# A scan's gate products put among its state updates, four norms' sums shared out anew, and a low half made earlier

## The chip, the cores and the metric

One kernel runs on one core of a Trainium2 chip. The metric is the device time of one execution in microseconds (us); lower is better. All work is in one launch. TensorE multiplies, VectorE, ScalarE and GpSimd do the elementwise work, and SyncE issues the large loads.

## The reference, cut to what matters

The reference is a chain of two blocks on 256 tokens of width 1024, with a context of 256 tokens beside them. The first block has a token mixer (a gated linear scan in two directions and a long convolution, merged under gates) and a mixture of 32 experts. The second has two layers of a hybrid mixer with a squared-relu MLP. Norms stand between all of them:

```python
def rms_norm(x, g):
    xf = x.astype(F32)
    y = xf * lax.rsqrt(jnp.mean(xf * xf, axis=-1, keepdims=True) + EPS)
    return (y * g.astype(F32)).astype(x.dtype)

def gla_chunk_scan(q, k, v, log_f, s0):          # in chunks of 32 tokens
    def step(S, xs):
        ...
        o = (jnp.einsum('bhtk,bhkv->bhtv', qc * jnp.exp(bc), S)
             + jnp.einsum('bhts,bhsv->bhtv', scores, vc))
        S_new = (jnp.exp(total[:, :, 0, :])[..., None] * S
                 + jnp.einsum('bhsk,bhsv->bhkv', kc * jnp.exp(total - bc), vc))
        return S_new, o

def merge_branches(y_a, y_b, g_logits, w_pa, w_pb, w_o):
    g_a, g_b = jnp.split(g_logits, 2, axis=-1)   # g_logits: part of h @ w_in
    mixed = jax.nn.sigmoid(g_a) * (y_a @ w_pa) + jax.nn.sigmoid(g_b) * (y_b @ w_pb)
    return mixed @ w_o
```

The scan has 4 heads of 128 and 8 chunks in each direction. The gate logits are 2048 of the columns of h @ w_in, which don't depend on the scan.

## The kernel before, in words

Five engine programs are written out by hand and are ordered by semaphores alone. At the end of each of fourteen stages every engine drains and waits for the others (`phase_end`). Weights come in chunks of 2 MB (512 columns or rows) through a ring of four slots; SyncE loads a chunk into a slot once TensorE has said that the slot's last chunk was used, and TensorE waits for a chunk with `chunk_in`. An fp32 matmul of the trace is two records. Where a product is needed in full precision from cheaper passes, both operands are split into a high and a low half (`mm3`: high x high, high x low, low x high).

*The scan* (stage `scan_b`, lines 740 to 797). For each of two directions d, TensorE turns the keys, makes scores (which VectorE masks out of banks 6 and 7 into SC, semaphore `masked`) and the context state (copied by VectorE, L2145, semaphore `states_out`). Then two halves bi follow, of four chunks each. A half begins with its state updates: for each chunk j a group of four matmuls on the 32 rows of this chunk, rows 32j to 32j + 31, into bank j. In the first half the products of masked scores and values follow (the "intra" products). Then for each chunk n the query product with the state before it (128x32, semaphore `inter`) waits until VectorE has made that state (L2153, L2154, `states_out`), and four products of a gate tile follow it (`gate_part`, 128 rows by 256 columns, banks 6 and 7). The gate tiles of a direction are 4 tiles of 8 products. In the second direction VectorE also does a part of the short convolution between two states (L2132 to L2134).

*The norms.* A norm (`mean_root`, then `norm`) needs the sum over the eight 128-row blocks of the squares. ScalarE squares a block once its residual has been added (L1380, semaphore `squares`). GpSimd adds blocks 1 to 5 into block 0 (`add_squares`, L1847, semaphore `squares_added`), and `sums` on TensorE multiplies blocks 0, 6 and 7 with a matrix of ones. Call 0 is the first norm; calls 1, 4, 5, 6 and 7 are the first block's second norm, layer 0's second, layer 1's first and second, and the final one. Calls 0, 4 and 5 are 512 wide, the others 256. TensorE's sums are followed by a stage end, except in the last call, where they precede the output.

*The low half.* In layer 1 the first two weight chunks of the input projection are split ahead: ScalarE copies four high halves (L1826) between its squares at the end of layer 0, VectorE makes the first chunk's two low halves there (L2627), and the second chunk's two low halves (L2417) behind the whole norm of layer 1, before it goes on to split the third chunk. TensorE waits for them at the second projection (`chunk_in(n + 1)`).

Of the kernel before, what the change touches and what calls it, by code (L numbers as in the profile page):

```python
# [30 lines left out]
L = 256  # L31
# [120 lines left out]
def build(nc, T, out):  # L152
    ctx = ExitStack()
    with ctx:
# [372 lines left out]
        W1h_cols, W2h_rows = W1h.rearrange("p (k n) -> p k n", k=KT), W2h.rearrange("p (k n) -> p k n", k=4)  # L527

        AHEAD = 3
        REST = [(k, 0) for k in range(AHEAD)] + [(k, s) for k in range(AHEAD, KT) for s in (1, 0)]  # L530
# [26 lines left out]
        def _(pe):  # L557
# [28 lines left out]
            def chunk_in(n, turns=0):  # L586
                pe.wait_ge(full[n % RING], arrived(n) + turns)
# [16 lines left out]

            def sums(call, nth, n, bank=6):

                pe.wait_ge(S("squares_added"), 5 * nth)
                for k in (0, KT - 2, KT - 1):
                    if k:
                        pe.wait_ge(S("squares"), 8 * call + k + 1)  # L610
                    mm(ps[bank][:, 0:n], ones, H[:, k, 0:n], k == 0, k == KT - 1, "sum_ready" if k == KT - 1 else None)
# [51 lines left out]
            ada_turn(1, 7, 1)  # L663
            sums(0, 1, 2 * L, 1)
            ada(2, 2, 6, blk=0)
# [73 lines left out]
            for d in range(2):  # L739
# [24 lines left out]
                for h in range(HG_H):  # L764
                    for tb in range(2):
                        mm(ps[0][:, h * P:(h + 1) * P], KDN[:, tb * 4 + h, :], Vn[:, 2 + tb, h * P:(h + 1) * P], tb == 0, tb == 1,
                           "ctx_state" if (h, tb) == (3, 1) else None)

                chunk_in(win(8 + d))
                pe.wait_ge(S("turned_out"), 4 * d + 4)  # L770
                pe.wait_ge(S("states_out"), 8 * d + 1)
                for bi in range(2):
                    tb = bi if d == 0 else 1 - bi
                    if bi:
                        pe.wait_ge(S("states_out"), 8 * d + 5)
                    for j in range(4):
                        r = slice(32 * j, 32 * j + 32)
                        for h in range(HG_H):
                            mm(ps[j][:, h * P:(h + 1) * P], KEN[r, tb * 4 + h, :], Vn[r, tb, h * P:(h + 1) * P],
                               inc="updates" if (j, h) == (3, 3) else None)  # L780
                    if bi == 0:
                        pe.wait_ge(S("masked"), 2 * d + 2)
                        for h in range(HG_H):
                            for tb2 in range(2):
                                mm(ps[4 + h // 2][:, (h % 2) * L + tb2 * P:(h % 2) * L + (tb2 + 1) * P],
                                   Vn[:, tb2, h * P:(h + 1) * P], SC[d][:, tb2 * 4 + h, :], False, False)
                    for c in range(4):
                        n = 4 * bi + c
                        ch = n if d == 0 else 7 - n
                        pe.wait_ge(S("states_out"), 8 * d + n + 1)  # L790
                        for h in range(HG_H):
                            mm(ps[4 + h // 2][:, (h % 2) * L + ch * 32:(h % 2) * L + ch * 32 + 32],
                               ST[:, n % 4, h * P:(h + 1) * P], QD[d][:, h, ch * 32:ch * 32 + 32], False, False,
                               "inter" if h == 3 else None)
                        gate_part(8 + d, n // 2, range(4 * (n % 2), 4 * (n % 2) + 4))
                chunk_used()
# [85 lines left out]
            for t in range(2, KT):  # L882
# [5 lines left out]
                if t % 4 == 3:  # L888
                    chunk_used()
            sums(1, 2, L)  # L890
            phase_end(pe, "merged")
# [157 lines left out]
            for l, first, mlp in ((0, L0, MLP0), (1, L1, MLP1)):  # L1049
# [215 lines left out]
                for t in range(2, KT):  # L1265
# [5 lines left out]
                    if t % 4 == 3:  # L1271
                        chunk_used()
                sums(ncall, 3 + 2 * l, W)
                ncall += 1
# [72 lines left out]
                flush()  # L1347
                sums(ncall, 4 + 2 * l, W)
                ncall += 1
# [483 lines left out]
        def _(pool):  # L1833
# [7 lines left out]
            def add_squares(call, n):  # L1841
                for k in range(1, KT - 2):
                    pool.wait_ge(S("squares"), 8 * call + k + 1)
# [112 lines left out]
        def _(dve):  # L1956
# [399 lines left out]
            with dve.If(more > 0):  # L2356
                with dve.Fori(0, more) as q:
                    dve.wait_ge(S("over_begun"), q * NX + 1)
                    V.tensor_scalar(RKM, RKM, -float(CAP), None, ALU.add).then_inc(S("over_ranked"), 1)
                    with dve.Fori(0, NX) as e:  # L2360
# [8 lines left out]
                        V.tensor_copy(SWT[0:CAP, :], ps[4][0:CAP, 0:L]).then_inc(S("over_weights"), 1)  # L2369
            dve.wait_ge(S("experts_done"), 1)  # L2370
            def split_chunk(n, c=KT * 512):

# [34 lines left out]
            for l in range(LAYERS):  # L2407
                W = 2 * L if l == 0 else L
                first = (L0, L1)[l]
                if l:  # L2410
                    norm(ncall, 1 + l, 0, (0, 1))
                    ncall += 1
                    n = L1 + 2
                    for a in range(2):
                        s = slice(2048 * a, 2048 * (a + 1))
                        dve.wait_ge(S("high_copied"), 12 + 2 + a + 1)
                        i = V.tensor_tensor(low(n)[:, s], slot(n)[:, s], NEXTh[2 + a].bitcast(F32), ALU.subtract)  # L2417
                    i.then_inc(full[(n + 1) % RING], 16)
                for j in range(1 + l, 5):
# [228 lines left out]
                if l == 0:  # L2648
# [3 lines left out]
                    link(V.tensor_tensor(mod[:, 2, 6:48, :], mod[:, 2, 6:48, :], bc(vecs[:, lo + 6:lo + 48].unsqueeze(2), [P, 42, 2]), ALU.add))  # L2652
                    gains(2)
                    phase_end(dve, "l0_mlp")
            dve.wait_ge(S("rms_ready"), ncall + 1)
# [64 lines left out]
```

## Time and profile before

| | us |
|---|---|
| median of 3 runs | 1965.12 (1961.49 to 1965.41) |
| the profiled execution | 1964.91 |
| its span, first to last instruction | 1963.1 |
| TensorE busy, share | 1869.2, 95% |
| VectorE busy, share | 817.9, 42% |
| ScalarE busy, share | 586.2, 30% |
| GpSimd busy, share | 389.0, 20% |

The stages that the change touches lie at 218 to 298 us (the scan), and the norms' sums at 402, 1183, 1544, 1763 and 1955 us. The stretch from about 440 to 870 us belongs to the experts, where the DMA engines move 427 GB/s. PEclk is the granted TensorE clock: 1.00 is 2.4 GHz and 0.50 is 1.2 GHz. A row of the timeline is start, duration, engine, line, operation, operands and count; a bracket behind it is the idle time of the engine before it and what ended that.

### The profile page before, as it was taken

What the parts mean: (1) busy time and instruction counts of PE and PEld (TensorE: products, weight loads), DVE (VectorE), ACT (ScalarE), POOL (GpSimd) and SP (SyncE); (2) the same over time, 40 slices, a digit from 0 to 9 for tenths busy, and PEclk for the clock granted to TensorE, in tenths of its full rate; (3) what the DMA queues carried; (4) which work ended last, traced back from release to release, by engine and by line L of the source; (5) the groups of instructions that cost most, each with busy time, mean ns of one, the idle gap of its engine ahead of it and who ended that gap; (6) DMA issues with size and microseconds to landing.
All of it is one profiled execution on the core that took longest, in us unless ns stands there. A gap on an engine that the chain in (4) does not pass through costs nothing.

```text
span 1963.1 us, 26165 instructions
## 1 busy us (share of the span) xinstructions
PE 1869.2 (95%) x11248; PEld 1369.8 (70%) x11248; DVE 817.9 (42%) x1342; ACT 586.2 (30%) x892; POOL 389.0 (20%) x205
## 2 busy tenths in 40 slices
PE   6999999999999999989999899999999899889998
PEld 2777796964443443437887657888888688779998
DVE  2625245731111111116342844556555625574333
ACT  2523103331111111114112535222333411544554
POOL 2000000120000000006002032433343250025665
PEclk9999999989999999999999999999999899999999
DMA  9569817569999999992224004345444232414551
GB/s 358 181 241 363 313 44 278 204 264 428 427 427 427 428 426 427 427 413 94 86 86 141 23 33 171 140 166 188 150 150 152 92 122 87 174 53 163 175 198 37
DMA packets 111425, 429.84 MB, mean 219 GB/s; under 512 B 5706, under 2 KB 8821, under 8 KB 98512
## 3 DMA queue, kind: packets, MB, share of 16 engines
q1 hardware_dynamic: 109056, 416.56, 54.7%
q0 software_dynamic: 2256, 11.62, 1.6%
q8 instruction: 90, 1.47, 0.3%
q14 instruction: 23, 0.19, 0.0%
HBM read 427.11 MB, written 1.05 MB: 218 GB/s over the span
## 4 chain that ended last, share of the span: by engine, by line
PE 66%; DMA 16%; DVE 6%; PEld 5%; ACT 3%; issue 3%; PEldq 0%; POOL 0%; SPq 0%; POOLq 0%; DVEq 0%; ACTq 0%
PE bank L562 65%; DMA ring<-in_moe_w_down 7%; PEld bank L562 5%; DMA H<-in_moe_w_down 4%; DMA arena<-in_moe_w_down 4%; PE bank L577 1%; DVE H L1989 1%; DVE H_low L1996 1%; PEldq L541 0%; DMA ring<-in_w_in 0%; DMA arena<-in_hy_filt_w 0%; DVE arena L2514 0%; DVE ring_low L2590 0%; DVE ring_low L2171 0%; DVE ring_low L2584 0%
## 5 line engine op out<-in xcount | busy, mean ns | idle before, releaser
L562 PE MATMUL bank<-arena_r 128*128 128x256 f32 (+1 forms) x2176 | 592.0, 339 | 12.0 <-ACT arena_r L1386 6.5
L562 PE MATMUL bank<-arena_r,ring_low 128*128 128x512 f32 (+2 forms) x1920 | 596.5, 342 | 1.7 <-DVE H_low L1996 1.0
L562 PEld LDWEIGHTS bank<-arena_r 128*128 128x128 f32 x2176 | 385.1, 190 | 63.8 <-issue 15.9
L562 PE MATMUL bank<-arena 128*128 128x64 bf16 (+8 forms) x2892 | 366.7, 320 | 39.9 <-DMA arena<-in_hy_filt_w 11.5
L562 PEld LDWEIGHTS bank<-arena_r,ring_low 128*128 128x128 f32 (+1 forms) x1920 | 352.7, 188 | 47.6 <-issue 2.7
L562 PEld LDWEIGHTS bank<-arena 128*128 128x128 bf16 (+4 forms) x2892 | 207.5, 133 | 199.8 <-issue 170.7
L562 PE MATMUL bank<-H_low,arena_r 128*128 128x512 f32 (+1 forms) x672 | 217.1, 340 | 0.0
L562 PE MATMUL bank<-ring,arena 128*64 128x512 f32 x768 | 170.2, 599 | 8.5 <-DMA ring<-in_moe_w_down 8.5
L2572 DVE SCALAR_TENSOR_TENSOR X<-bank,mod,X 128x256 f32<-128x256 f32 x216 | 94.2, 478 | 196.6 <-PE bank L562 196.6
L1928 POOL TENSOR_TENSOR ring_low<-ring,arena_r 128x2048 fp32r<-128x2048 f32 x31 | 142.4, 4614 | 131.2 <-DVE ring_low L2584 68.8
L1400 ACT ACTIVATE arena<-bank 128x512 f32<-128x512 f32 (+2 forms) x106 | 51.2, 496 | 368.1 <-PE bank L562 367.9
L2344 DVE SCALAR_TENSOR_TENSOR arena_r<-bank,arena,arena_r 128x512 fp32r<-128x512 f32 x32 | 24.0, 750 | 307.2 <-ACT arena_r L1586 307.2
L1944 POOL TENSOR_TENSOR arena_r<-arena,arena_r 128x512 fp32r<-128x512 f32 (+1 forms) x64 | 104.6, 1647 | 222.4 <-ACT arena L1806 222.4
L562 PEld LDWEIGHTS bank<-ring,arena 128*64 128x64 f32 x768 | 56.5, 138 | 115.1 <-issue 115.0
L562 PEld LDWEIGHTS bank<-H_low,arena_r 128*128 128x128 f32 x672 | 125.5, 192 | 14.3
L2640 DVE SCALAR_TENSOR_TENSOR arena<-ring,arena 128x1024 f32<-128x1024 f32 x84 | 99.5, 1222 | 66.0 <-POOL arena_r L1944 62.5
L562 PE MATMUL bank<-H,arena 128*64 128x512 f32 (+4 forms) x464 | 118.0, 436 | 7.4 <-DVE arena L2530 2.8
L562 PE MATMUL bank<-X,ring 128*128 128x256 f32 x512 | 118.1, 386 | 0.0
L562 PEld LDWEIGHTS bank<-X,ring 128*128 128x128 f32 x512 | 96.5, 192 | 17.8 <-issue 4.7
L1799 ACT ACTIVATE arena_r<-ring 128x4096 fp32r<-128x4096 f32 x15 | 54.5, 3631 | 172.4 <-DMA ring<-in_w_mlp 123.3
L562 PE MATMUL bank<-H_low,ring_low 128*128 128x512 f32 (+2 forms) x272 | 93.4, 358 | 0.0
L1884 POOL CAST ring_low<-ring 128x4096 fp32r<-128x4096 f32 x1 | 3.6, 3598 | 450.5 <-DMA ring<-in_w_in 450.5
(326 smaller groups left out, 1939.3 us busy)
## 6 DMA issues: line engine op xcount, KB each, us to landing
ring<-in_w_mlp SPq DMA_DIRECT2D x32, 2048.0 KB, 7.9
ring<-in_w_in SPq DMA_DIRECT2D x26, 2048.0 KB, 8.9
ring<-in_ada_w SPq DMA_DIRECT2D x24, 2048.0 KB, 12.2
ring<-in_moe_w_up SPq DMA_DIRECT2D x17, 2048.0 KB, 23.2
ring<-in_moe_w_gate SPq DMA_DIRECT2D x17, 2048.0 KB, 27.9
arena<-in_moe_w_up SPq DMA_DIRECT2D x15, 2048.0 KB, 22.5
ring<-in_moe_w_down SPq DMA_DIRECT2D x14, 2048.0 KB, 23.4
arena<-in_moe_w_down SPq DMA_DIRECT2D x13, 2048.0 KB, 23.5
```

Source lines behind the costliest of these rows:

```text
L562: ins = nc.tensor.matmul(o, l, r, start=start, stop=stop, skip_group_check=True)
L577: ins = nc.tensor.transpose(o, i, ident)
L1400: A_(o, i, f, **kw).then_inc(S("tile_free"), 1)
L1799: A_(W2h, slot(n), ACT.Copy).then_inc(S("w_high"), 1)
L1884: G.tensor_copy(low(L0 + 1), slot(L0)).then_inc(S("pool_ready"), 1)
L1928: G.tensor_tensor(low(n)[:, s], slot(n)[:, s], W1h[:, s].bitcast(F32), ALU.subtract).then_inc(S("w1_split"), 1)
L1944: G.tensor_tensor(HAl[:, nt, 0:W], HA[:, nt, 0:W], HAh[:, nt, 0:W].bitcast(F32), ALU.subtract)\
L1989: V.scalar_tensor_tensor(H[:, k, c], X[:, k, c], gsc[:, b, which, k, s:s + 1], root[:, c], ALU.mult, ALU.mult)\
L1996: return V.scalar_tensor_tensor(Hl[:, k, c], H[:, k, c], mod[:, b, 24 * which + k, s:s + 1], high[:, k, c].bitcast(F32), ALU.add, ALU.subt ...
L2344: V.scalar_tensor_tensor(YSl[:, s], ps[6 + nb][:, :], WSL, YSh[:, s].bitcast(F32), ALU.mult, ALU.subtract)\
L2572: i = V.scalar_tensor_tensor(X[:, t, s * L:(s + 1) * L], o[:, s * L:(s + 1) * L], mod[:, 1 + l, gate + t, s:s + 1], X[:, t, s * L:(s + 1) ...
L2640: d = V.scalar_tensor_tensor(CPROD[:, c, :], as_turned(n)[:, q % 3, :], 1.0, CSIL[:, c, :], ALU.mult, ALU.mult, accum_out=mod[:, 2, bass.d ...
```

## The change

Three things change. In the scan the gate products of a direction are handed out by an iterator in the same order as before: two ahead of the wait for the first state (behind the chunk's arrival and the wait for the mask, which moves up), one behind each of the four groups of updates of a half, and three or two (not four) behind each query product. In all calls of the sums but the first, GpSimd adds blocks 1 to 3 instead of 1 to 5, and TensorE sums blocks 0, 4, 5, 6 and 7. In layer 1, one low half of the second chunk is made by VectorE at the end of layer 0 (behind the gains, before the stage end), and the other ahead of the norm instead of behind it.

```diff
+        def blocks_added(call):
+            return KT - 2 if call == 0 else KT - 4
+        def added_before(call):
+            earlier = {0: (), 1: (0,), 4: (0, 1), 5: (0, 1, 4), 6: (0, 1, 4, 5), 7: (0, 1, 4, 5, 6)}[call]
+            return sum(blocks_added(c) - 1 for c in earlier)
...
-            def sums(call, nth, n, bank=6):
-                pe.wait_ge(S("squares_added"), 5 * nth)
-                for k in (0, KT - 2, KT - 1):
+            def sums(call, n, bank=6):
+                m = blocks_added(call)
+                pe.wait_ge(S("squares_added"), added_before(call) + m - 1)
+                for k in (0, *range(m, KT)):
                     if k:
                         pe.wait_ge(S("squares"), 8 * call + k + 1)
                     mm(ps[bank][:, 0:n], ones, H[:, k, 0:n], k == 0, k == KT - 1, "sum_ready" if k == KT - 1 else None)
...
+                gates = iter([(nt, k) for nt in range(4) for k in range(KT)])
+                def gate_products(m):
+                    for _ in range(m):
+                        nt, k = next(gates)
+                        gate_part(8 + d, nt, (k,))
                 chunk_in(win(8 + d))
+                pe.wait_ge(S("masked"), 2 * d + 2)
+                gate_products(2)
                 pe.wait_ge(S("turned_out"), 4 * d + 4)
                 pe.wait_ge(S("states_out"), 8 * d + 1)
                 for bi in range(2):
...
                         for h in range(HG_H):
                             mm(ps[j][:, h * P:(h + 1) * P], KEN[r, tb * 4 + h, :], Vn[r, tb, h * P:(h + 1) * P],
                                inc="updates" if (j, h) == (3, 3) else None)
+                        gate_products(1)
                     if bi == 0:
-                        pe.wait_ge(S("masked"), 2 * d + 2)
...
-                        gate_part(8 + d, n // 2, range(4 * (n % 2), 4 * (n % 2) + 4))
+                        gate_products(3 if n < 6 else 2)
...
             def add_squares(call, n):
-                for k in range(1, KT - 2):
+                for k in range(1, blocks_added(call)):
...
+            def next_low(a):
+                s = slice(2048 * a, 2048 * (a + 1))
+                dve.wait_ge(S("high_copied"), 12 + 2 + a + 1)
+                return V.tensor_tensor(low(L1 + 2)[:, s], slot(L1 + 2)[:, s], NEXTh[2 + a].bitcast(F32), ALU.subtract)
...
                 if l:
+                    next_low(1).then_inc(full[(L1 + 3) % RING], 16)
                     norm(ncall, 1 + l, 0, (0, 1))
                     ncall += 1
-                    n = L1 + 2
-                    for a in range(2):
-                        s = slice(2048 * a, 2048 * (a + 1))
-                        dve.wait_ge(S("high_copied"), 12 + 2 + a + 1)
-                        i = V.tensor_tensor(low(n)[:, s], slot(n)[:, s], NEXTh[2 + a].bitcast(F32), ALU.subtract)
-                    i.then_inc(full[(n + 1) % RING], 16)
...
                     gains(2)
+                    next_low(0)
                     phase_end(dve, "l0_mlp")
```

The callers of `sums` lose their `nth` argument.

## Rows read from the trace of the kernel before

**Rows 1.** The page: TensorE's busy time, and its granted clock in 40 slices.
```profile
PE 1869.2 (95%) x11248; PEld 1369.8 (70%) x11248; DVE 817.9 (42%) x1342; ACT 586.2 (30%) x892; POOL 389.0 (20%) x205
...
PEclk9999999989999999999999999999999899999999
```

**Rows 2.** The page: the chain that ended last, by engine.
```profile
PE 66%; DMA 16%; DVE 6%; PEld 5%; ACT 3%; issue 3%; PEldq 0%; POOL 0%; SPq 0%; POOLq 0%; DVEq 0%; ACTq 0%
```

**Rows 3.** TensorE's timeline in the scan: start, us, what, count [idle before, releaser].
```profile
229.91 2.79 PE L562 MATMUL bank<-arena 32*128 32x128 f32 x32 [0.87 <-DVE arena L2145]
...
236.95 1.97 PE L562 MATMUL bank<-X,ring 128*128 128x256 f32 x8
...
263.47 1.95 PE L562 MATMUL bank<-H 128*128 128x128 f32 x16
...
284.54 0.38 PE L562 MATMUL bank<-X,ring 128*128 128x256 f32 x1
284.85 2.82 PE L562 MATMUL bank<-arena 32*128 32x128 f32 x32
287.59 1.08 PE L562 MATMUL bank<-H,arena 128*128 128x32 f32 x8
288.51 1.97 PE L562 MATMUL bank<-X,ring 128*128 128x256 f32 x8
...
288.81 0.38 PE L562 MATMUL bank<-X,ring 128*128 128x256 f32 x1
```

**Rows 4.** TensorE's waits in the scan: total us, times, longest.
```profile
PE bank L562 <- DVE arena L2145: 1.7, 2, 0.9
```

**Rows 5.** Stretches: us, PE busy, PEld, DVE, ACT, POOL, granted clock, DMA share, GB/s.
```profile
233.00:236.50 3.50, 3.50 (x19) 3.50 (x19) 3.19 (x6) 0.00 (x0) 0.00 (x0) 0.51 1.05 388
...
250.10:253.60 3.50, 3.50 (x11) 2.96 (x11) 3.22 (x6) 0.00 (x0) 0.00 (x0) 0.51 0.00 0
...
270.60:274.00 3.40, 3.40 (x17) 3.18 (x16) 2.84 (x6) 0.00 (x0) 0.00 (x0) 0.50 0.12 40
274.00:298.20 24.20, 24.20 (x164) 21.94 (x162) 15.86 (x30) 1.15 (x3) 0.00 (x0) 1.00 0.00 1
```

**Rows 6.** Timeline of VectorE: the last state of the second direction.
```profile
294.10 0.69 DVE L2154 TENSOR_TENSOR arena<-arena,bank 128x512 f32<-128x512 f32 x1
```

**Rows 7.** TensorE's timeline: the sums of the first block's second norm.
```profile
402.00 1.03 PE L562 MATMUL bank<-H,base 128*128 128x256 f32 x4
403.19 0.70 PE L562 MATMUL bank<-H,base 128*128 128x256 f32 x2 [0.16 <-ACT H L1380]
```

**Rows 8.** TensorE's timeline: the sums of layer 0's second norm.
```profile
1182.74 2.92 PE L562 MATMUL bank<-H,base 128*128 128x512 f32 x6
```

**Rows 9.** Timelines of all engines about layer 1's first norm.
```profile
1542.30 1.65 ACT L1380 ACTIVATE H<-X 128x512 f32<-128x512 f32 x3
1543.00 1.27 POOL L1847 TENSOR_TENSOR H<-H 128x512 f32<-128x512 f32 x1 [1.05 <-ACT H L1380]
...
1544.32 4.26 PE L562 MATMUL bank<-H,base 128*128 128x512 f32 x6 [3.27 <-POOL H L1847]
...
1550.13 1.67 DVE L1989 SCALAR_TENSOR_TENSOR H<-X,gsc,RS 128x256 f32<-128x256 f32 x4 [7.60 <-ACT RS L1377]
...
1562.81 4.48 DVE L2417 TENSOR_TENSOR ring_low<-ring,arena_r 128x2048 fp32r<-128x2048 f32 x2
...
1567.39 0.47 PE L562 MATMUL bank<-arena_r 128*128 128x512 f32 x1 [1.50 <-DVE ring_low L2417]
```

**Rows 10.** The stretch in which the first projection of layer 1 begins.
```profile
1550.60:1557.40 6.80, 5.70 (x27) 5.73 (x28) 6.80 (x19) 4.43 (x10) 0.00 (x0) 0.50 0.00 1
```

**Rows 11.** Timelines about layer 1's second norm.
```profile
1762.78 1.56 PE L562 MATMUL bank<-H,base 128*128 128x256 f32 x6 [0.40 <-POOL H L1847]
...
1765.49 0.47 ACT L1376 ACTIVATE RS<-bank,vecs 128x256 f32<-128x256 f32 x1 [2.14 <-DVEq L541]
```

**Rows 12.** TensorE's timeline: the sums of the final norm.
```profile
1954.62 1.62 PE L562 MATMUL bank<-H,base 128*128 128x256 f32 x6
```

More of the change, by code:

```diff
@@ L663, in _ @@
             ada_turn(1, 7, 1)
-            sums(0, 1, 2 * L, 1)
+            sums(0, 2 * L, 1)
             ada(2, 2, 6, blk=0)
@@ L889, in _ @@
                     chunk_used()
-            sums(1, 2, L)
+            sums(1, L)
             phase_end(pe, "merged")
@@ L1272, in _ @@
                         chunk_used()
-                sums(ncall, 3 + 2 * l, W)
+                sums(ncall, W)
                 ncall += 1
@@ L1347, in _ @@
                 flush()
-                sums(ncall, 4 + 2 * l, W)
+                sums(ncall, W)
                 ncall += 1
```

## The prediction

> **What bounds the kernel now.** I read the page's busy table and its forty slices first: TensorE works in 95% of the span, at the full clock in nearly every slice [rows 1]. The chain of waits agrees: 66% of it is TensorE, 16% is DMA, most of it in the experts' stage, which is not touched [rows 2]. So a saving counts where TensorE either waits or runs at the lower clock, and a cost counts where it adds passes or breaks the packing of its passes. Everything between the scan and the experts is ordered by semaphores from TensorE's own progress, the loads included (a slot is loaded once it is used), and so is what follows; I let every shift pass through to the end. In the trace each fp32 matmul is two records, which I call passes.
>
> **The scan, the largest part.** Four blocks of state updates (two directions, two halves) have 32 passes each on 32 rows, in four groups of eight, one group for each row quarter. The change puts one gate product (two passes, 128 rows, 256 columns) behind each group.
>
> *Packing.* Passes of one kind come every 0.11 us where they can't overlap: the sixteen score passes take 1.95 us less the last one's 0.28, over fifteen intervals. Thirty-two would then need 31 x 0.111 = 3.45 us from the first start to the last, and a start behind passes of another kind adds 0.1 (as 288.51 to 288.81 for the first two gate passes, where the later ones stand 0.215 apart: 288.81 to 288.51 + 1.97 - 0.38 = 290.10, six intervals). The block takes less: it starts at 284.85 and its last pass starts at 284.85 + 2.82 - 0.27 = 287.40, so 2.55 us. The difference, 1.0 us, is three boundaries between groups at 0.33 us: the next quarter's first passes run beside the last ones of the quarter before. A full-height gate product between them leaves nothing to run beside. On top of that each change between 32 and 128 rows costs time in both directions: the last gate pass starts at 284.54 and the first update at 284.85, 0.31 us instead of 0.215; from the last update at 287.40 to the next 128-row pass it is 0.19; and the first gate pass to the second takes 0.30 [rows 3]. One group followed by one product, up to the next group, is therefore 0.88 (seven intervals and the slower start) + 0.19 + 0.30 + 0.31 = 1.68 us; now a group inside a block takes 2.55 less 0.88, over three = 0.56, and a product 0.43, together 0.99. Each of the three inner insertions costs 0.7 us, the fourth nothing (the change of height is there already). Four blocks: 12 x 0.7 = **+8.4 us**. The bounds are 0 (if the products slip in as they do among themselves) and 12 x 0.8; I take the value of the rows, since both transitions stand in them.
>
> The Trainium skill speaks against the change here: TensorEngine Tiling (Array Packing), Key Properties, says that different tiles can load and multiply in parallel, and that changing the tiling mode makes TensorE drain. By this rule every change pays a drain; the trace agrees with its 0.31 and 0.19 us.
>
> *Idle time.* Before the first block of each direction TensorE waits for the first state to be copied, 0.87 us twice [rows 3, 4]. Two products (0.95 us) now stand there. The mask they must wait for is made while TensorE still computes the context state, and the chunk's wait stood here already; behind both waits on TensorE are the updates, for which VectorE waits, and they start no later than now. **-1.7 us.**
>
> *The clock.* Three stretches of 3.4 us are at 1.2 GHz, each right behind a block of updates: granted clock 0.51, 0.51 and 0.50; about the fourth block it is 1.00 [rows 5]. From the first update of the first block to its first gate pass it takes 7.04 us (229.91 to 236.95), against 2.74 (284.85 to 287.59) + 1.88 (16 passes of 128 columns, with a slower start) + 0.82 (287.59 to 288.51 less 0.1) = 5.44 at the full clock [rows 3]: 1.6 us lost; I use it for each of the three. If the clock stays up this is **-4.8 us**. It should: the mix of gate passes and light 128x32 passes behind 274 never loses the clock, nor does the fourth block at 284.85, which directly follows a run of gate products; and the new block has two full-height passes for eight updates throughout. It is not certain, for this mix stands in no row and lies between those that kept the clock and those that lost it.
>
> The skill's TensorE: Matmul & The Clock Gate, Why this matters for your kernels, ties throughput drops to long idle gaps between bursts. By that alone the scan has nothing to regain, since TensorE is busy through the low stretches with at most 0.87 us of idle time ahead of them, and the sum would be 4.8 us higher. The trace disagrees: the clock falls after low-row work with no idle time.
>
> *The states.* VectorE builds the states of the second direction with a convolution between them; the last is ready at 294.10 + 0.69 = 294.79, 7.4 us behind the last update pass [rows 3, 6]. TensorE now reaches the last state after 0.2 + 0.5 (product four) + 3 x 0.83 (inter passes) + two runs of three products at 1.38 and one of two at 0.95 = 6.9 us. It will wait some 0.5 us. **+0.5 us.** Earlier states are in time, since the block's end signal, the states and the queries behind it all shift together.
>
> Scan: 8.4 - 1.7 - 4.8 + 0.5 = **+2.4 us**.
>
> **The norms.** In the five later norms GpSimd adds three squares instead of five, TensorE sums five blocks instead of three: four passes more. It pays only where GpSimd is late.
> - *First block's second norm:* four passes run while square 7 is made, then two [rows 7]. Two of the four new passes fit before 403.19; the last pass moves from 403.51 to 402.00 + 9 x 0.215 = 403.94. **+0.4 us.**
> - *Layer 0, second norm (512 wide):* the six passes stand closely, the last starts at 1182.74 + 2.92 less its own 0.6, at 1185.07 [rows 8]; ten at 0.43 put it at 1186.6. **+1.5 us.**
> - *Layer 1, first norm:* here GpSimd is late. Its last add waits for square 5 and ends at 1544.27; TensorE idles 3.27 us and then starts cold: six passes in 4.26 us [rows 9]. Now the adds end before the last MLP tile does; blocks 0 and 4 go at once (from about 1541.1, where TensorE falls idle now), and 5, 6, 7 follow their squares (three in 1.65 us from 1542.30). Ten passes at 0.43, 0.1 for the start and the last one's tail end at about 1545.7, not 1548.58: 2.9 us earlier. The first low half (2.2 us, half of the row's 4.48) starts when VectorE is free, 7.60 us ahead of 1550.13, is ready at about 1544.8 and hides; the high copy that it reads is ahead of squares 5 to 7 on ScalarE. The second (2.2 us) starts with the new phase at 1545.8 and ends near 1548.1, later than the root (1547.3), so the norm starts at 1548.1 for 1550.13: 2.0 us earlier. The first projection ends 2.0 earlier too, at 1567.39 - 1.50 - 2.0 = 1563.9, and the second follows at once where it waited for the two low halves until 1567.39 [rows 9]: **-3.5 us**. Its bounds: -2 or less if the first half is late and holds the phase, and -5.2 if the low clock of this stretch (0.50 for 6.8 us [rows 10]) is halved.
> - *Layer 1, second norm:* the phase waits for VectorE's low half. ScalarE starts the root at 1765.49, released by VectorE, while the sums end at 1764.34 [rows 11]; four passes of 0.215 more end at 1765.2. **0**, and at the worst +0.9 us.
> - *Final norm:* nothing waits for GpSimd, and nothing hides the four passes: 4 x 0.215 less a short wait [rows 12]. **+0.8 us.**
>
> Norms: 0.4 + 1.5 - 3.5 + 0.8 = **-0.8 us**.
>
> **The sum.** 2.4 - 0.8 = +1.6 us on the profiled execution's 1964.91 (span 1963.1): 1966.5. The median of the runs shown, 1965.12, is 0.2 above it: **1966.7 us**, no change that can be told. What a measurement of this kernel can tell from no change is about 0.2%, or 3.9 us.
>
> **The rivals.**
> - *The clock stays low in the new blocks (slower).* Place: the four update blocks, now 6 us long each. Price: the 4.8 us are not regained and the fourth block loses 1.6 as well: +1.6 + 6.4 = +8.0, 1973 us; up to 1979 if a block holds two low stretches. It decides from the point where a group and its product, with the gaps of the two changes of height, no longer keep the granted clock at 1.00. For: those gaps are new. Against: the fourth block kept the clock with gate passes only ahead of it.
> - *The products cost little among the updates (faster).* Then the 8.4 us shrink: at a third of it (the transitions without the lost overlap) the total is +1.6 - 5.6 = -4.0, 1961 us; at nothing -6.8, 1958 us. The extra 1.7 us of the layer 1 stretch pulls the same way. Against: the overlap is in the trace and needs neighbouring quarters.
> - *The norm gains little.* The change does not do what it says if the first low half ends after TensorE's sums, or if GpSimd's three adds are late: then -3.5 becomes about -1 and the total +4.1, 1969 us. For: 1 us of slack only. Against: VectorE has been idle since 1542.5.
>
> **Numbers.** My forecast 0.45 (spread -2 to +4 about it), the low clock 0.22, cheap insertion 0.2, weak norm 0.13. The forecast itself spills a little over either bound: faster by over 0.2% is 0.17, within 0.2% 0.46, slower 0.37. The range 1959.5 to 1974 leaves out the far end of the low-clock case and of free insertion.
>
> **What would show it.** Groups of updates about 1.7 us apart with a product between, and a first block from first to last update near 5.9 us instead of 2.55; granted clock 1.00 throughout the scan; no wait for the copied first state and a short one for the last state of the second direction; the scan's end about 2 us later. In the norms: no idle of TensorE on GpSimd ahead of the layer 1 norm, and the second projection right behind the first. I am wrong if updates and products keep an interval near 1.0 us per pair, or if the clock row shows low stretches inside the blocks.

## The result, and the profile after

The changed kernel takes 1983.28 us (median of 4 runs, 1981.41 to 1985.54) against 1965.23 us before (1961.49 to 1965.41): a ratio of 1.0084, 95% interval 1.0061 to 1.0106, so 12 to 21 us slower. The forecast was 1966.7 us with a range up to 1974; the time lies outside it. The profiled execution has a span of 1983.2 us, 20.1 us more than before's 1963.1.

The page of the changed kernel: busy time, granted clock by slices, chain of waits [rows 1, 2].

```profile
PE 1897.0 (96%) x11268; PEld 1386.4 (70%) x11268; DVE 816.5 (41%) x1342; ACT 586.2 (30%) x892; POOL 378.8 (19%) x195
...
PEclk9999978989999999999999899999999999999999
...
PE 69%; DMA 15%; DVE 5%; PEld 5%; ACT 3%; issue 3%; PEldq 0%; POOL 0%; SPq 0%; ACTq 0%; DVEq 0%; POOLq 0%
```

TensorE has 20 passes more (1.8 thousandths of its passes) but 27.8 us more busy time, so its passes have become slower on the whole. The clock row says where: slices 6 and 7 (248 to 347 us) stand at 7 and 8, where 9 stood. I split the 20.1 us at events that both traces have. Up to the scan's first update -0.5; **the scan, from its first update to the first pass behind it, 87.24 us for 68.94: +18.3**; to the first block's second norm +0.1; through that norm and the experts +2.8; to layer 0's second norm +1.2; to layer 1's second norm (layer 1's first norm lies in it) -3.2; to the final norm +0.6; the rest +0.8.

The scan in TensorE's timeline (columns as [rows 3]; line 571 is before's line 562):

```profile
228.34 1.03 PE L571 MATMUL bank<-X,ring 128*128 128x256 f32 x4
229.38 1.12 PE L571 MATMUL bank<-arena 32*128 32x128 f32 x8
230.44 0.70 PE L571 MATMUL bank<-X,ring 128*128 128x256 f32 x2
231.07 1.15 PE L571 MATMUL bank<-arena 32*128 32x128 f32 x8
...
234.49 1.26 PE L571 MATMUL bank<-arena 32*128 32x128 f32 x8
235.68 1.22 PE L571 MATMUL bank<-X,ring 128*128 128x256 f32 x2
```

Two products stand ahead of the first block with no idle time, then a group comes every 1.71 us (231.07 to 234.49 is two periods). The product behind the fourth group takes 1.22 us for two passes that took 0.70 before: there the clock has fallen. The next view shows how much of the scan runs that way. Stretches of the changed kernel (columns as [rows 5]; the last one is the whole scan):

```profile
229.38:235.40 6.02, 6.02 (x38) 4.66 (x38) 0.00 (x0) 0.00 (x0) 0.00 (x0) 1.00 1.05 388
235.40:238.80 3.40, 3.40 (x15) 3.00 (x14) 2.76 (x4) 0.00 (x0) 0.00 (x0) 0.50 0.80 293
252.50:262.70 10.20, 10.20 (x36) 8.38 (x36) 4.14 (x6) 0.38 (x1) 0.00 (x0) 0.50 0.00 0
279.80:290.00 10.20, 10.20 (x41) 9.26 (x40) 8.58 (x16) 0.38 (x1) 0.00 (x0) 0.50 0.00 1
300.30:310.50 10.20, 10.20 (x36) 8.38 (x35) 5.34 (x10) 0.39 (x1) 0.00 (x0) 0.50 0.00 0
229.38:316.62 87.24, 86.72 (x460) 74.03 (x460) 30.52 (x53) 5.14 (x12) 0.00 (x0) 0.80 0.18 63
```

34.0 us of the scan are at the lower level (0.50, 1.2 GHz), where before it was 10.3 us [rows 5]; its mean clock is 0.80, and TensorE is busy in 86.72 of the 87.24 us. The blocks themselves hold the smaller part of this. These are the passes at the end of the second and of the third block and behind them:

```profile
254.31 2.07 PE L571 MATMUL bank<-arena 32*128 32x128 f32 x8
256.32 1.22 PE L571 MATMUL bank<-X,ring 128*128 128x256 f32 x2
257.33 1.75 PE L571 MATMUL bank<-arena 128*128 128x32 f32 x8
258.90 2.91 PE L571 MATMUL bank<-X,ring 128*128 128x256 f32 x6
...
280.90 1.22 PE L571 MATMUL bank<-X,ring 128*128 128x256 f32 x2
281.91 5.17 PE L571 MATMUL bank<-H,arena 128*128 128x128 f32 x24
286.89 2.91 PE L571 MATMUL bank<-X,ring 128*128 128x256 f32 x6
```

In each block the clock falls during the third or fourth group, or just behind the last update (at 235.40 in the first block). Up to the end of each block's fourth product (236.70, 257.33, 281.91 and 305.74) the low time adds up to about 14 us; the other 20 us run on through the intra products, the queries and the gate products that follow.

What TensorE waits for, from 225 to 320 us (columns as [rows 4]): no state any more, in place of before's 1.7 us.

```profile
PE bank L571 <- ACTq L550: 0.5, 1, 0.5
PE bank L571 <- DVE mod L1995: 0.5, 1, 0.5
PE bank L571 <- ACT arena L1532: 0.2, 1, 0.2
```

The sums of the five later norms, in order [rows 7, 8, 9, 11, 12]:

```profile
419.86 2.32 PE L571 MATMUL bank<-H,base 128*128 128x256 f32 x10
...
1204.62 4.45 PE L571 MATMUL bank<-H,base 128*128 128x512 f32 x10
...
1564.54 4.75 PE L571 MATMUL bank<-H,base 128*128 128x512 f32 x10
...
1781.47 2.32 PE L571 MATMUL bank<-H,base 128*128 128x256 f32 x10
...
1973.90 2.42 PE L571 MATMUL bank<-H,base 128*128 128x256 f32 x10
```

None waits for GpSimd, and the third one starts with no idle time, where before TensorE idled 3.27 us. About it, on VectorE and then on TensorE, the two low halves, the norm, and the second projection [rows 9]; the last row is ScalarE's root in layer 1's second norm [rows 11]:

```profile
1565.95 2.29 DVE L2394 TENSOR_TENSOR ring_low<-ring,arena_r 128x2048 fp32r<-128x2048 f32 x1
1569.44 2.29 DVE L2394 TENSOR_TENSOR ring_low<-ring,arena_r 128x2048 fp32r<-128x2048 f32 x1 [1.20 <-PEq L550]
1571.65 1.67 DVE L2008 SCALAR_TENSOR_TENSOR H<-X,gsc,RS 128x256 f32<-128x256 f32 x4
...
1586.58 0.47 PE L571 MATMUL bank<-arena_r 128*128 128x512 f32 x1 [0.21 <-ACT arena L1419]
...
1784.74 0.47 ACT L1395 ACTIVATE RS<-bank,vecs 128x256 f32<-128x256 f32 x1 [2.14 <-DVEq L550]
```

### The profile page after: what moved, and what is told of

It is laid out like the page before. It is cut to its first block, busy times and chain, and to the rows that moved or that the text cites. A ratio compares the mean times of both kernels' runs of the same rounds, so it can differ in the third digit from the quotient of the medians.

```text
span 1983.2 us, 26187 instructions
## 1 busy us (share of the span) xinstructions
PE 1897.0 (96%) x11268; PEld 1386.4 (70%) x11268; DVE 816.5 (41%) x1342; ACT 586.2 (30%) x892; POOL 378.8 (19%) x195
## 4 chain that ended last, share of the span: by engine, by line
PE 69%; DMA 15%; DVE 5%; PEld 5%; ACT 3%; issue 3%; PEldq 0%; POOL 0%; SPq 0%; ACTq 0%; DVEq 0%; POOLq 0%
PE bank L571 68%; DMA ring<-in_moe_w_down 7%; PEld bank L571 5%; DMA H<-in_moe_w_down 4%; DMA arena<-in_moe_w_down 3%; PE bank L586 1%; PEldq L550 0%; DMA ring<-in_w_in 0%; DMA arena<-in_hy_filt_w 0%; DVE arena L2534 0%; DVE ring_low L2610 0%; DVE H L2008 0%; DVE ring_low L2190 0%; DVE ring_low L2604 0%; DVE ring_low L2084 0%
## 5 line engine op out<-in xcount | busy, mean ns | idle before, releaser
L571 PE MATMUL bank<-arena 128*128 128x64 bf16 (+8 forms) x2892 | 381.4, 323 | 38.2 <-DMA arena<-in_hy_filt_w 11.7
L571 PEld LDWEIGHTS bank<-arena 128*128 128x128 bf16 (+4 forms) x2892 | 218.1, 135 | 205.2 <-issue 173.7
L571 PE MATMUL bank<-X,ring 128*128 128x256 f32 x512 | 128.5, 402 | 0.0
L571 PE MATMUL bank<-ring_low,arena_r 128*128 128x512 f32 x288 | 92.8, 394 | 0.0
```

The costliest lines, as they stand in the source:

```text
L571: ins = nc.tensor.matmul(o, l, r, start=start, stop=stop, skip_group_check=True)
```

## The experiments

The theory: the loss is the lower clock that one product per group lets in; packing costs what the prediction says. The rival: the insertions themselves cost more than foreseen, or a wait does. "The scan" below is always the stretch from the first update to the first pass behind the scan, in the run's one profiled execution, and whole times are medians. Numbers in brackets behind a ratio are its 95% interval. The comparison's kernel before had 1965.2 to 1966.0 us.

**The scan's part and the norms' part, each alone.** The first takes the hunks on the gate products, the second those on the sums and the low half; nothing else is edited.

> Only the scan's part of the change (products ahead, one behind each group, three or two behind each query); norms and low halves as before. Theory A (the low clock inside the update blocks carries the loss; the lost packing is the 0.7 us per inner insertion that the forecast had): about 17 us slower than before, with 7 to 10 stretches of 3.4 us at 1.2 GHz between the first update and the scan's end, and groups of updates 1.7 us apart wherever the clock is full. Rival B (the loss comes from the norms or from the experts' stage, which took 2 us more in the changed kernel): below 10 us slower.

> Only the sums and the low halves; the scan as before. Theory A: faster by 1 to 3 us (+0.4, +1.5, -4 to -5, 0, +0.8 as the trace of the changed kernel has them). Rival B: slower by 2 us or more, because the four added passes cost in five places and the gain of layer 1 is undone later. The experts' stage (last pass of the first block's second norm to the transposes behind the experts) within 1 us of before if its 2.4 us in the changed kernel were chance; 2 us longer if the later sums cause them.

The scan's part alone: 1983.54 us, ratio 1.0079 (1.0051 to 1.0107), scan 87.24 us, the same to a hundredth. The norms' part alone: 1963.76 us, 0.9994 (0.9978 to 1.0010), scan 68.95 us. The whole loss is in the scan. Its stretch with the scan's part alone:

```profile
231.51:318.75 87.24, 86.72 (x461) 74.08 (x461) 30.52 (x53) 5.14 (x12) 0.00 (x0) 0.80 0.17 63
```

**Two products behind each group, and none.** The kernel is the one with the scan's part alone (the norms as before), and only the counts change:

```diff
-                        gate_products((1, 1, 1, 1)[j])
+                        gate_products((2, 2, 2, 2)[j])
...
-                        gate_products((3, 3, 3, 3, 3, 3, 2, 2)[n])
+                        gate_products((2, 2, 2, 2, 2, 2, 1, 1)[n])
```

The other kernel has no product inside a block, and (4, 4, 4, 4, 4, 4, 3, 3) behind the queries.

> The scan's part alone, but two gate products behind each group instead of one (2 ahead, 8 in each half, then two, at the end one, behind each query). The lost packing is the same as with one product: 12 inner insertions of 0.7 us. Theory A (what was mis-sized is the clock: one product a group is too little to keep it, two are enough): granted clock 1.00 through the scan, a period of 2.1 us from group to group, and the scan about 2 to 4 us longer than before, total within 1 to 5 us of before. Rival B (products among low-row passes bring the clock down whatever their number): low stretches in the blocks as with one product, 10 us or more slower than before.

> The scan with whole update blocks as before; only two gate products stand ahead of the first state's wait, and four or three follow each query. Theory A: the 0.87 us waits of TensorE go (-1.7 us) and nothing else is lost; the clock behind the blocks falls in about as many places as before, so -2 us, with 1.6 us more or less for each low stretch fewer or more. Rival B (the early wait for the mask or the later queries cost the gain): no change or slower.

With two products behind each group: 1972.20 us, 1.0023 (1.0007 to 1.0039). With none: 1962.82 us, 0.9988 (0.9971 to 1.0005). Both scans as stretches, two products first:

```profile
231.61:305.49 73.88, 72.08 (x460) 61.42 (x460) 30.54 (x53) 5.14 (x12) 0.00 (x0) 0.98 0.21 74
```

```profile
231.05:293.37 62.32, 61.81 (x460) 56.85 (x460) 30.52 (x53) 5.14 (x12) 0.00 (x0) 1.00 0.25 88
```

Sixteen more products among the updates make the scan 13.4 us shorter, and the clock is at 1.00 through all four blocks (it falls once, at the scan's last 3 us). There are twelve inner interruptions as in the change, so it isn't the number of interruptions. The scan is still 4.9 us longer than before's 68.94, where 2 to 4 were expected, and the median is 7.0 us above before's, where 1 to 5 were expected: TensorE waits 1.22 us for the last state here, and behind this wait come the low 3 us. With no product inside, the profiled scan has no low stretch and is 6.6 us shorter than before's, but the median is only 2.4 us lower, with 1 inside the interval.

**The same product twice.** The scan's part alone, and each product inside a block is added in twice (so the gates come out otherwise). The second argument of `gate_products` is the number of times that each product is issued:

```diff
-                        gate_products((1, 1, 1, 1)[j])
+                        gate_products(1, 2)
```

> The scan's order of the changed kernel, nothing else of the change, and each of the sixteen products behind a group of updates is done twice (it is added in twice, so that the gates come out otherwise): 32 passes more, 16 x 0.43 = 6.9 us of work added. Theory A, the loss is the lower clock that one product per group lets in (ten stretches of 3.4 us in the scan, in place of three): with two products' worth of full-height work behind each group the clock stays at 1.00 in the scan as it does with two different products there, the period of group and products is 2.14 us, and the scan takes 18 us less than now in low stretches x one half = about -14 + 6.9 = 6 to 8 us less than with single products: about 1976 us, though it does more. Rival B, the loss is a price per insertion or a wait that has nothing to do with the clock: the extra work comes on top, 1983.5 + 6.9 = about 1990 us.

1978.91 us, 1.0067 (1.0044 to 1.0090). This is the cleanest case, for nothing is moved and work is only added:

```profile
231.30:309.51 78.21, 77.69 (x493) 66.76 (x493) 30.55 (x53) 5.14 (x12) 0.00 (x0) 1.00 0.19 69
```

With 32 passes more the scan is 9.0 us shorter than with single products (78.21 against 87.24), and its clock 1.00 against 0.80. The rival's 1990 us is excluded. The expected 1976 was 3 us too good: the whole time fell by 4.6 us, less than the scan, and the intervals of the two ratios overlap. In the profiled execution the stage of the experts took 499.2 us where it took 494.8 with single products, which is told of below. So the clock's part is read from the scan of the profiles; the whole times alone don't show it here.

**Two interruptions of which one is inside the block.** The scan's part alone, with the four products of a block in pairs behind groups two and four:

```diff
-                        gate_products((1, 1, 1, 1)[j])
+                        gate_products((0, 2, 0, 2)[j])
```

> Two products ahead of the first block as in the change, but the four of a block stand in pairs behind the second and the fourth group: one interruption inside a block instead of three. If each inner interruption costs 0.7 us at the full clock, and the clock holds: 4 x 0.7 - 1.7 (the wait for the first state filled) - 4.8 (three low stretches gone) = -3.7 us, about 1961.5 us, and a block lasts 2.55 + 0.7 + 0.86 = 4.1 us. If what counts is how much light work stands between full-height passes, sixteen updates in a row could let the clock fall again: three or four stretches of 3.4 us, +1.7 us each, about 1965 to 1968 us. If a price per product rather than per interruption held, the scan would be as long as with 2, 2, 2, 2 products, 4.9 us above the kernel before.

1961.02 us, 0.9974 (0.9959 to 0.9989), scan 65.50 us, clock 1.00. A block in TensorE's timeline:

```profile
229.56 1.68 PE L562 MATMUL bank<-arena 32*128 32x128 f32 x16
231.17 1.13 PE L562 MATMUL bank<-X,ring 128*128 128x256 f32 x4
232.23 1.71 PE L562 MATMUL bank<-arena 32*128 32x128 f32 x16
```

From its first update to its last it takes 4.11 us: the undisturbed 2.52 (2.79 less 0.27 for the last pass, [rows 3]), 0.86 for the product pair, and 0.73 for one interruption. Against the kernel with none inside (62.32) the scan is 3.2 us longer for four interruptions, 0.8 each; the doubled products give (78.21 - 62.32 - 16 x 0.43) / 12 = 0.75. The price of an interruption was near the forecast 0.7.

**The loops exchanged.** If a boundary between quarters saves time because passes of different rows run side by side, every boundary should. In the kernel before:

```diff
-                    for j in range(4):
-                        r = slice(32 * j, 32 * j + 32)
-                        for h in range(HG_H):
+                    for h in range(HG_H):
+                        for j in range(4):
+                            r = slice(32 * j, 32 * j + 32)
```

> The kernel before with only the two loops of the updates exchanged: head outside, row quarter inside, so that neighbouring passes are always in different quarters. If the overlap that is seen at the three boundaries between groups (0.33 us each) holds between all passes, a block goes from 2.55 us to between 1.0 and 1.7 us: four times -0.9 to -1.5, and with the shorter light stretches one or more of the three low stretches may go (1.6 us each): 1955 to 1962 us. Rival: the overlap is one of a boundary only (the end of one run of accumulations beside the start of the next), or the passes are bound by their issue; then the block stays at 2.5 us and the time at 1965.

1954.65 us, 0.9937 (0.9913 to 0.9960); the profiled execution was the slowest of its six, 1961.30 us. A block, and the scan:

```profile
276.53 1.17 PE L562 MATMUL bank<-arena 32*128 32x128 f32 x32
```

```profile
231.35:288.89 57.54, 56.16 (x465) 51.25 (x465) 30.58 (x53) 5.14 (x12) 0.00 (x0) 1.00 0.26 94
```

The thirty-two updates take 0.90 us from first to last (276.53 + 1.17 less 0.27 for the last pass) where they took 2.55, on average a pass every 0.03 us, better than any bound I had given. Pass by pass the trace has four starts within 0.02 us, one in each quarter (276.74, 276.75, 276.75, 276.76), and the next four from 276.85 on: a quarter still takes a pass every 0.11 us, and the four run beside each other. None of the low stretches is left, though one profile of unchanged code has none either (last section). The same exchange in the whole changed kernel:

> The changed kernel whole, with only the two loops of the updates exchanged (head outside, row quarter inside), so that one product stands behind eight updates as before, but each eight are spread over the four quarters. The thirty-two updates then took 0.90 us from first to last instead of 2.55, 0.03 apart. Eight of them and a product should take 7 x 0.03 + 0.19 + 0.30 + 0.31 = about 1.0 to 1.1 us instead of 1.71, and there is no overlap between groups left to lose. Theory A (the loss is the low clock, and that comes with long stretches of light passes between few full-height ones): no low stretches in the scan, -17 us, and four blocks 2.5 us shorter, -10: scan 18.3 - 27 = 9 us shorter than in the kernel before, time about 1955 us; against the quarters alone the insertions still cost 12 x 0.25 to 12 x 0.5 us. Rival B (one product behind each group of eight brings the low clock whatever the group's length): only the 10 us come off, about 1973 us.

1957.41 us, 0.9955 (0.9939 to 0.9972), scan 61.43 us at 1.00:

```profile
233.34 0.50 PE L571 MATMUL bank<-arena 32*128 32x128 f32 x8
233.78 0.70 PE L571 MATMUL bank<-X,ring 128*128 128x256 f32 x2
234.41 0.50 PE L571 MATMUL bank<-arena 32*128 32x128 f32 x8
```

The period is 1.07 us as expected. With the same sixteen products, one behind each eight updates, 25.8 us of the scan are gone, and the changed kernel is faster than the one before. What loses is one product between long light groups, not a product between updates as such. The insertions still cost 5.6 us (61.43 against 55.81 in the last kernel below).

**The norm of layer 1.** One kernel takes of the norms' part only this norm (GpSimd adds three squares there, the low half is made ahead), the other only the low half made ahead.

> Of the norms' part only the first norm of layer 1: GpSimd adds three squares there instead of five, TensorE sums seven blocks less two, and the low half is made ahead. If the steps measured in the changed kernel hold alone (-2.9 us to the sums' end, and the norm and its second projection behind them), -3.5 to -5 us: 1960 to 1962 us, and 1 to 3 us less than with all five norms changed, whose other four cost 0.4 + 1.5 + 0 + 0.8. Rival: the gain is used up by an extra low stretch of the clock behind the shortened norm; then 1964 to 1965.

> Only the low half made ahead of the norm of layer 1, all adds on GpSimd as before. The sums still end where they do, VectorE has nothing to do before them, and the norm's start is bound by the root and the second half low. If the norm starts then 1 to 2 us earlier and its second projection waits no more for the low halves (1.5 us in the kernel before), about -2 to -2.5 us: 1962.5 to 1963.5. If the sums alone make the gain, 1965.

The first: 1960.47 us, 0.9978 (0.9963 to 0.9993), as expected. The second: 1966.51 us, 1.0005 (0.9990 to 1.0019), a miss. GpSimd's last two adds and VectorE's first low half in it:

```profile
1541.13 1.28 POOL L1847 TENSOR_TENSOR H<-H 128x512 f32<-128x512 f32 x1 [2.56 <-ACT H L1380]
1543.45 3.01 POOL L1847 TENSOR_TENSOR H<-H 128x512 f32<-128x512 f32 x1 [1.04 <-ACT H L1380]
...
1543.05 2.29 DVE L2375 TENSOR_TENSOR ring_low<-ring,arena_r 128x2048 fp32r<-128x2048 f32 x1
```

The last add takes 3.01 us beside the low half and 1.27 without it [rows 9], so TensorE's sums, which wait for it, start 1.7 us later, and this eats the gain. So the low half pays ahead of the norm only where GpSimd adds less. Fewer adds without the low half were not run.

**All that pays, together.** The exchanged loops, two products ahead of the first block, none inside, and of the norms only layer 1's first:

> What the experiments point to, together: updates with the quarter as the inner loop, two products ahead of the first block of each direction, none inside a block (4, 4, 4, 4, 4, 4, 3, 3 behind the queries), and of the norms' part only the first norm of layer 1, with TensorE summing four blocks more there and the low half made ahead. From the run with two products ahead alone (scan 6.6 us shorter) the quarters would take 4 to 6 us more and the norm 3.5: a span of about 1957.6 - 5 - 3.5 = 1949 us. Rival: the exchanged loops do nothing and the norm's gain is within what executions differ by: 1955 to 1958 us.

1946.73 us (1943.83 to 1949.92), ratio 0.9899 (0.9875 to 0.9922): 1% faster than the kernel before and 1.8% faster than the changed one.

```profile
232.59:288.40 55.81, 55.30 (x460) 50.33 (x460) 30.53 (x53) 5.13 (x12) 0.00 (x0) 1.00 0.27 98
```

## Why the prediction was wrong

**Packing was right.** 1.68 us a period was forecast and 1.71 came; the first block takes 5.99 us from first to last update (forecast 5.9); an inner interruption costs 0.73 to 0.8 us (forecast 0.7), so twelve cost about 9.0 where the sum had 8.4.

**Idle time was right.** Both waits for the first state are gone. The kernel with products ahead and none inside has a scan of 62.32 us; the unchanged scan at the full clock takes 64.06 us (below), so they were worth 1.7 us.

**The states' +0.5 us is not seen in the change.** There the low clock delays TensorE. Among the kernels whose clock is up in the blocks, the doubled products and the pairs have no wait for the last state, the exchanged change 0.5 us, and two products behind each group 1.22 us. What the wait would be in the change at the full clock no run shows.

**The step that failed is "The clock".** It said -4.8 us: three low stretches regained. In place of 10.3 low us there were 34.0. The sum goes like this. The scan with its products inside, at the full clock, would be 62.32 + 12 x 0.75 = 71.3 us, an estimate, 7.3 more than 64.06; the prediction's terms for all but the clock were 8.4 - 1.7 + 0.5 = 7.2. That they meet so closely is partly luck: 0.6 too little for the interruptions and 0.5 for a wait that this sum doesn't have. The kernel with two products agrees with the estimate: 73.88 less the 1.22 of waiting and 1.4 for its low 3.0 us (at the 0.47 worked out next) is 71.3. Measured is 87.24, so the clock costs 15.9 us, 0.47 us for each of the 34.0 low ones. In the kernel before it cost 68.94 - 64.06 = 4.9 us over 10.3, again 0.47. So +18.3 = 7.3 + 15.9 - 4.9, where the forecast had 7.2 + 0 - 4.8.

The fault was in the reading of [rows 5]. I took the fourth block, with the clock at 1.00 about it, as evidence for the new blocks. But that row has one block of 2.8 us directly behind eight passes of gate products, while the new blocks have four groups with one product each. I said myself that this mix stands in no row, and then gave the outcome on the other side 0.22. I also under-priced that rival: one low stretch in each block, or 1979 us with two; with three of the four blocks came 10.2 us each. Its point of decision was right: a group and its product no longer keep the clock. Its place was only half right: about 20 of the 34.0 us lie behind the blocks, in passes that the kernel before runs mostly at the full clock. Why the clock stays down for 10.2 us at three blocks and for 3.4 at the first the runs don't show; the first and the third are followed by the same passes. One candidate is that three products stand behind each query where four stood. They don't make the clock fall, for the kernels with doubled products and with pairs have three there too and keep 1.00; whether they lengthen a low stretch was not run.

The -4.8 us had a second weakness: they were read from one execution. The scan of the kernel before stands unchanged in four profiles, and it has three low stretches in two of them, one in the third and none in the fourth (last section). So the low stretches that were to be regained are not there in every execution.

TensorE is never idle in these stretches (10.20 us busy of 10.20). The Trainium skill's TensorE: Matmul & The Clock Gate, Why this matters for your kernels, ties such drops to idle gaps between bursts; the trace doesn't agree, and the doubled products and the exchanged loops keep the clock up without taking a wait away. What it is about the light passes that counts, the runs don't tell, and I leave it open.

**The norms.** Layer 1's first norm was forecast at -3.5 with -5.2 as an end; between layer 0's second norm and layer 1's second it came to -3.2 in spite of +1.5 for the sums in it, so -4.7. This stretch has 6.8 us less of low clock, which is part of it; how large a part was not measured by itself. The low half ran where it was put, the second one bound the norm's start as forecast (1569.44 + 2.2 = 1571.65), and the second projection waits 0.21 us where it waited 1.50. The first block's norm (last pass +0.43), layer 0's second (+1.53) and the final one (+0.8) came as forecast. Layer 1's second was put at 0 and cost 0.6: the ScalarE root starts 3.27 us behind the sums' first pass, 2.71 before [rows 11]. With all, -1.4 for the forecast -0.8, read from two profiles; the median with the norms' part alone can't be told from before's.

**The rest,** +2.8 us in the experts' stage and +1.2 behind it, was no term of the sum. 0.4 of it is the norm's four passes. No kernel here edits the experts' stage; in the profiles it takes 494.0 to 494.8 us in seven of them, with 27 to 31 us at the lower clock, and 496.8 to 499.2 in six others, with 31 to 34 us. The low time doesn't sort them by itself: with 30.7 low us it took 494.8 us with the scan's part alone and 496.8 in the exchanged change. I take the rest for a difference between executions, but its cause is not shown.

## What to carry to other kernels

Price a new mix of passes from a row in which that mix runs for as long as it will run, and where there is none, give the other outcome of TensorE's clock its full chance and its full length, and look for it behind the new mix as well as in it. Passes on 32 rows want their neighbours in other row quarters; exchanging two loops did more here than any placement of filler work, and with the loops exchanged a single product behind each eight updates left the clock at 1.00. In the old order one product at a time did not, and two at a time did. When work is moved from a wait into an engine's idle time, look at what its neighbour engine does in that time.

## What the runs showed of the hardware

- Updates on 32 rows in four different quarters start within 0.03 us of each other, in the same quarter 0.11 us apart; 32 of them take 0.90 us with the quarter as the inner loop and 2.55 with it as the outer one. Changing between 32-row and 128-row passes cost 12 x 0.47 us with the loops exchanged too (61.43 less 55.81).
- The clock of unchanged code differs between executions. In the profile of the kernel with only the low half ahead, the scan is before's, instruction for instruction, and has no low stretch, where before's profile has three:

```profile
231.14:295.20 64.06, 62.67 (x465) 57.77 (x465) 30.56 (x53) 5.13 (x12) 0.00 (x0) 1.00 0.24 86
```

  This gives the 64.06 us used above. Its whole time was none the better for it (1964.93 us for the profiled execution): other stages had more low stretches. The other two profiles with this scan have 68.95 us (the norms' part alone, three low stretches) and 65.65 (only layer 1's norm, one). So a gain of a few us in one profile's clock isn't a gain in the median.
- A 128x512 add on GpSimd took 3.01 us beside a VectorE operation with two SBUF inputs, 1.27 alone. It started at 1543.45, the VectorE operation ended at 1545.34, and 1545.34 + 1.27 = 1546.61 is near its end at 1546.46. This agrees with the Trainium skill's SBUF — State Buffer, SBUF: two separate sides, by which one of the two holds the shared ports for a whole instruction and the other is blocked.
